# A fused two-block kernel: its modulation front in one piece per channel tile, sums by transposes, parameters loaded later

## The reference

```python
c_act = jax.nn.silu(c)
mod = (c_act @ w_mod[l] + b_mod[l])[:, None, :]
sh1, sc1, g1, sh2, sc2, g2 = jnp.split(mod, N_MOD, axis=-1)
h = rms_norm(x) * (1.0 + sc1) + sh1
proj = h @ w_in[l]
```

## Time and profile before

| | |
|---|---|
| median of 3 runs | 1368.52 us (1367.58 to 1370.42) |
| profiled execution: its time | 1368.94 us |
| profiled execution: span, first to last instruction | 1367.6 us |
| TensorE busy | 1354.0 us (99%) |
| VectorE, ScalarE, GpSimd busy | 896.1, 629.1, 241.8 us |
| DMA moved, mean | 163.46 MB, 120 GB/s |
| mean granted TensorE clock | 0.999 |

### The profile page before, as it was taken

The page is one execution under the profiler, slowest core; times in us unless marked ns, Lnnn a source line. Parts: engine busy times, 40 slices in busy tenths (PEclk is TensorE's granted clock), DMA queues, the critical chain, the costliest instruction groups (busy, mean ns, idle before and its releaser), DMA issues.

```text
span 1367.6 us, 24510 instructions
## 1 busy us (share of the span) xinstructions
PE 1354.0 (99%) x9502; PEld 1094.6 (80%) x9502; DVE 896.1 (66%) x1274; ACT 629.1 (46%) x1000; POOL 241.8 (18%) x254
## 2 busy tenths in 40 slices
PE   8999999999999999999999999999999999999998
PEld 5788888888887888878888888888888877777776
DVE  4687877887658867775668543234444687777865
ACT  4566556565555522332245441223333465545533
POOL 0000000000028889770022600000000000000320
PEclk9999999999999999999999999999999999999999
DMA  9444444444455676463333333333333232223221
GB/s 347 131 141 138 118 123 131 120 127 124 143 142 154 159 205 206 146 177 92 93 93 92 108 93 105 96 93 92 96 105 92 73 106 67 80 60 93 64 74 77
DMA packets 276009, 163.46 MB, mean 120 GB/s; under 512 B 6573, under 2 KB 264242, under 8 KB 275898
## 3 DMA queue, kind: packets, MB, share of 16 engines
q1 hardware_dynamic: 269530, 158.90, 40.1%
q10 hardware_dynamic: 6368, 3.00, 0.8%
HBM read 159.59 MB, written 2.29 MB: 118 GB/s over the span
## 4 chain that ended last, share of the span: by engine, by line
PE 89%; DVE 4%; ACT 2%; issue 2%; POOL 2%; DMA 1%; ACTq 0%; SPq 0%; DVEq 0%; POOLq 0%
PE PS L742 23%; PE PS L744 22%; PE PS L743 22%; PE PS L942 1%; PE PS L1354 1%; PE PS L1019 1%; PE PS L1021 1%; PE PS L1020 1%; POOL mbuf L607 1%; PE PS L963 1%; PE PS L1355 1%; PE PS L1356 1%; PE PS L1257 1%; PE PS L1268 1%; POOL mbuf L602 1%
## 5 line engine op out<-in xcount | busy, mean ns | idle before, releaser
L742 PE MATMUL PS<-Hh,whi 128*128 128x512 f32 x1096 | 443.1, 404 | 1.0 <-DVE wlo L2114 0.5
L744 PE MATMUL PS<-Hh,wlo 128*128 128x512 f32 x1096 | 427.7, 390 | 0.0
L743 PE MATMUL PS<-Hl,whi 128*128 128x512 f32 x1096 | 427.3, 390 | 0.0
L2114 DVE TENSOR_TENSOR wlo<-raw,whi 128x1024 fp32r<-128x1024 f32 (+2 forms) x211 | 275.7, 1307 | 119.3 <-ACT whi L1457 118.5
L1457 ACT ACTIVATE whi<-raw 128x1024 fp32r<-128x1024 f32 (+2 forms) x215 | 222.6, 1036 | 168.7 <-PE PS L744 119.0
L742 PEld LDWEIGHTS PS<-Hh,whi 128*128 128x128 f32 x1096 | 205.8, 188 | 49.9 <-issue 6.2
L744 PEld LDWEIGHTS PS<-Hh,wlo 128*128 128x128 f32 x1096 | 205.7, 188 | 44.4
L743 PEld LDWEIGHTS PS<-Hl,whi 128*128 128x128 f32 x1096 | 206.1, 188 | 39.6 <-issue 0.7
L602 POOL TENSOR_TENSOR mbuf<-mbuf,cact 128x1024 f32<-128x1024 f32 x32 | 67.1, 2097 | 409.6 <-DMA mbuf<-in_w_mod_dram 403.6
L607 POOL TENSOR_TENSOR mbuf<-mbuf 128x512 f32<-128x512 f32 x68 | 101.8, 1497 | 5.3
L742 PE MATMUL PS<-YBh,whi 128*128 128x512 f32 x256 | 99.6, 389 | 0.0
(11 more groups left out here) (484 smaller groups left out, 1957.9 us busy)
## 6 DMA issues: line engine op xcount, KB each, us to landing
raw<-in_w_in_dram SPq DMA_DIRECT2D x106, 512.0 KB, 3.9
raw<-in_w_ff_dram SPq DMA_DIRECT2D x64, 512.0 KB, 3.7
mbuf<-in_w_mod_dram SPq DMA_DIRECT2D x32, 512.0 KB, 3.9
crow<-cum_rows SPq DMA_DIRECT2D x32, 256.0 KB, 4.4
...
```

What stands on the lines that cost most here:

```text
L742: pe.matmul(bank[:, :], whi[s][:, k, :], xh[:, kk, :], start=kk == 0, stop=False)
L743: pe.matmul(bank[:, :], whi[s][:, k, :], xl[:, kk, :], start=False, stop=False)
L744: last = pe.matmul(bank[:, :], wlo[s][:, k, :], xh[:, kk, :], start=False, stop=t == end - 1 and k == (order or range(kt))[-1])
L2114: v.tensor_tensor(wlo[s][:, 0:kt, :], raw[s][:, 0:kt, :], whi[s][:, 0:kt, :].bitcast(F32), ALU.subtract).then_inc(s_wlo, 1)
```

## The change

- The columns of `w_mod` are loaded in eight pairs, one per channel tile m: `wm[m]` takes the 128 scale columns and the 128 shift columns of tile m, two loads of 128 columns each. `mod_rows(m)` takes both in one go, 256 wide, eight times (before: four times 128 and six times 256).
- `mod_sums(m)` turns both halves of `mrow` by two transposes; VectorE adds the four partial sums by a reduction over 4 of the columns that it picks (partitions 0, 32, 64, 96 of before), into two new columns of `small`, and then makes `opc` and `modc` for one channel tile. `selc` and its three GpSimd instructions fall away.
- At the start ScalarE issues only `c` and `b_mod`, without a wait between, and runs one Silu on a constant ahead of that of `c`. The other five loads of `fill1` go to SyncE, ahead of the ten of `fill2`, behind the last landing of `wm`. Their transposes and copies stand at the end of the front.
- The order on TensorE, ScalarE and VectorE is written anew: 10 fillers at the start become 4, all four chunks of x are turned in one go, the first `mod_rows` waits until x is copied whole, the parts of channel tile m - 1 stand around `mod_rows(m + 1)` and so on. `lo(2)` stands behind `h_scaled(2)`. The last parts are one channel tile's for each of the three tiles (before: two channel tiles').
- The unused filler tensor and its GpSimd copies go; `small` grows by as much as `selc` took with its padding, and all other buffers keep their places. Waits on shared semaphores are counted anew.

The diff, cut to its core (left out are the waits that were only counted anew):

```diff
-    selc = sb("selc", [P, 2])
...
-    small = sb("small", [P, 64])
+    small = sb("small", [P, 72])
...
-    N_PAR2 = 16 * 10
+    N_BMOD, N_PAR2 = 16, 16 * 16
...
-    MOD_ROWS = [(i, at, 128) for at in (0, 128) for i in (4, 0)] + [(j + i, 0, 256) for j in range(1, 4) for i in (4, 0)]
-    of_cols = lambda m: m if m < 2 else m // 2 + 1
...
-        def load_mod0(i, at, n):
-            if at:
-                sp.wait_ge(s_x[i // 4], 16)
-            sp.dma_start(wm[i][:, :, at:at + n], cols(W_MOD, i * 256 + at, n)).then_inc(s_wmr[i // 4] if at else s_wm[i], 16)
+        def load_mod0(m):
+            for j in (1, 0):
+                sp.dma_start(wm[m][:, :, j * 128:j * 128 + 128], cols(W_MOD, j * D + m * 128)).then_inc(s_wm[m], 16)
 
         for c in range(NC):
             load_x(c)
-        for p, piece in enumerate(MOD_ROWS):
-            load_mod0(*piece)
-            if p in (1, 3, 5):
-                load((1, 3, 5).index(p))
-
-        sp.wait_ge(s_wm[3], 16)
-        for to, ap in fill2:
+        for m in range(KT):
+            load_mod0(m)
+            if m < 3:
+                load(m)
+
+        sp.wait_ge(s_wm[7], 32)
+        sp.wait_ge(s_par2, N_BMOD)
+        for to, ap in fill1[2:] + fill2:
...
-        def keep_busy_rounded(n, width, bank=5):
-            for i in range(n):
-                pe.matmul(BK[bank][:, 0:width], filler[:, i % 2 * 128:i % 2 * 128 + 128], filler[:, 0:width],
-                          start=True, stop=True)
-
-        def keep_busy_half(n, bank=5):
+        def keep_busy_half(n, bank=2):
+            pe.wait_ge(s_const, 6)
...
-                    pe.wait_ge(s_pc, 3)
+                    pe.wait_ge(s_cact, 1)
...
-        keep_busy(4, 0)
         pe.wait_ge(s_par, 16)
         pe.transpose(BK[5][:, 0:8], pr[1][0:8, :], ident[0:8, 0:8]).then_inc(s_pt, 1)
-        keep_busy(6, 0)
-        x_turned(0)
-        x_turned(1)
-        pe.wait_ge(s_par, 16 * 7)
-        pe.wait_ge(s_cact, 1)
-        pe.transpose(BK[5][:, 128:256], pr[1][:, :], ident[:, :]).then_inc(s_pt, 1)
-        x_turned(2)
-        x_turned(3)
-
-        def mod_rows(n):
-            i, at, width = MOD_ROWS[n]
-            if n >= 2:
-                pe.wait_ge(s_mrow, n - 1)
-            pe.wait_ge(*((s_wmr[i // 4], 32) if at else (s_wm[i], 16)))
+        keep_busy(4, 0)
+        for c in range(NC):
+            x_turned(c)
+
+        def mod_rows(m):
+            if m >= 2:
+                pe.wait_ge(s_mrow, m - 1)
+            pe.wait_ge(s_wm[m], 32)
             for k in range(KT):
                 q = 32 * (k % 4)
-                ms = pe.matmul(BK[3 + n % 2][q:q + 32, 0:width], cact[:, k:k + 1].to_broadcast([P, 32]),
-                               wm[i][:, k, at:at + width], start=k < 4, stop=k >= 4)
+                ms = pe.matmul(BK[3 + m % 2][q:q + 32, 0:256], cact[:, k:k + 1].to_broadcast([P, 32]), wm[m][:, k, :],
+                               start=k < 4, stop=k >= 4)
             ms.then_inc(s_mt, 1)
 
-        def mod_sums(n):
-            pe.wait_ge(s_mrow, n + 1)
-            if n >= 2 and n % 2 == 0:
-                pe.wait_ge(s_modc, n)
-            for to, at in [(2 * (n % 2) + n // 2, 0)] if n < 4 else [(2 * n - 4, 0), (2 * n - 3, 128)]:
-                ms = pe.matmul(BK[6][:, to:to + 1], mrow[n % 2][:, at:at + 128], selc[:, 0:1], start=True, stop=True)
+        def mod_sums(m):
+            pe.wait_ge(s_mrow, m + 1)
+            if m > 0:
+                pe.wait_ge(s_modc, 2 * m)
+            for j in range(2):
+                ms = pe.transpose(BK[6][:, j * 128:j * 128 + 128], mrow[m % 2][:, j * 128:j * 128 + 128], ident[:, :])
             ms.then_inc(s_ms, 1)
...
+        pe.wait_ge(s_xt1, 2)
+        pe.wait_ge(s_par2, N_BMOD)
+        pe.transpose(BK[5][:, 128:184], pr[1][0:56, :], ident[0:56, 0:56]).then_inc(s_pt, 1)
+        pe.wait_ge(s_xt0, 6)
+        keep_busy_half(4)
+        mod_rows(0)
+        keep_busy_half(3)
+        mod_sums(0)
+        keep_busy_half(5)
         mod_rows(1)
-        pe.wait_ge(s_xt1, 2)
-        keep_busy(2, 5)
-        mod_sums(0)
+        part(0, 0)
         mod_sums(1)
-        keep_busy_half(6)
+        keep_busy_half(9)
         mod_rows(2)
-        keep_busy_half(3)
-        mod_rows(3)
-        pe.wait_ge(s_xt0, 6)
-        part(0, 0)
-        mod_sums(2)
-        mod_sums(3)
-        keep_busy_half(9)
         part(1, 0)
         part(0, 1)
+        mod_sums(2)
         part(1, 1)
+        part(2, 0)
+        mod_rows(3)
+        part(2, 1)
+        mod_sums(3)
+        part(0, 2)
+        part(1, 2)
         mod_rows(4)
+        part(2, 2)
+        mod_sums(4)
+        part(0, 3)
+        part(1, 3)
         mod_rows(5)
-        keep_busy_half(2)
-        mod_sums(4)
+        part(2, 3)
         mod_sums(5)
-        keep_busy_half(4)
-        part(2, 0, 1)
+        part(0, 4)
+        part(1, 4)
         mod_rows(6)
-        part(0, 2, 3)
+        part(2, 4)
+        mod_sums(6)
+        part(0, 5)
+        part(1, 5)
         mod_rows(7)
-        part(1, 2)
-        mod_sums(6)
+        part(2, 5)
         mod_sums(7)
-        part(1, 3)
-        part(2, 2, 3)
-        mod_rows(8)
-        part(0, 4)
-        mod_rows(9)
-        part(0, 5)
-        mod_sums(8)
-        mod_sums(9)
-        part(1, 4, 5)
-        part(2, 4, 5)
+        part(0, 6)
+        part(1, 6)
+        part(2, 6)
         pe.wait_ge(s_par2, N_PAR2)
-        pe.transpose(BK[3][:, :128], pr[0][:, :], ident[:, :]).then_inc(s_pt, 1)
+        pe.transpose(BK[3][:, 0:128], pr[0][:, :], ident[:, :]).then_inc(s_pt, 1)
+        pe.transpose(BK[3][:, 128:256], pr[1][:, :], ident[:, :]).then_inc(s_pt, 1)
         pe.transpose(BK[4][:, :rC], pr[2][0:rC, :], ident[0:rC, 0:rC]).then_inc(s_pt, 1)
         for t in range(3):
-            part(t, 6, 7)
+            part(t, 7)
...
-        act.wait_ge(s_par, 16)
-        for to, ap in fill1[1:]:
-            act.dma_start(to, ap).then_inc(s_par, 16)
+        act.dma_start(*fill1[1]).then_inc(s_par2, 16)
+        act.wait_ge(s_pc, 1)
+        act.activation(small[:, 63:64], EPS, ACTF.Silu)
...
-        mod_row(0)
-        mod_row(1)
-        hi(0)
-        h_hi(0)
-        mod_row(2)
-        mod_row(3)
-        hi(1)
-        h_hi(1)
-        mod_row(4)
-        mod_row(5)
-        hi(2)
-        for j in range(1, 4):
-            h_hi(2 * j)
-            h_hi(2 * j + 1)
-            for n in ((6, 7), (8, 9), ())[j - 1]:
-                mod_row(n)
+        for m in range(KT):
+            mod_row(m)
+            if m < 3:
+                hi(m)
+            h_hi(m)
...
-        for b in range(2):
+        for b in range(4):
             x_copy(b, 0)
-        v.wait_ge(s_pt, 2)
-        cols_of(BK[5][:, 128:256], pcB, 128, 1.0)
-        for b in range(2, 4):
-            x_copy(b, 0)
-        x_copy(0, 1)
         v.wait_ge(s_rx, 5)
         v.reciprocal(small[:, 4:8], small[:, 4:8]).then_inc(s_xrs, 1)
+        x_copy(0, 1)
         x_copy(2, 1)
-
-        def h_cols(i):
-            m, n = (i, 1) if i < 2 else (2 * i - 2, 2)
-            at = m if i < 2 else 2 * m
-            v.wait_ge(s_ms, 2 * i + 2)
-            v.scalar_tensor_tensor(out=opc[:, m:m + n], in0=BK[6][:, at:at + n], scalar=1.0,
-                                   in1=colr("b_mod", 8 + m, n), op0=ALU.add, op1=ALU.add).then_inc(s_modc, 1)
-            v.tensor_tensor(modc[:, m:m + n], BK[6][:, at + 2:at + 2 + n], colr("b_mod", m, n),
-                            ALU.add).then_inc(s_modc, 1)
+        v.wait_ge(s_pt, 2)
+        cols_of(BK[5][:, 128:184], pcB, 56, 1.0)
+
+        def h_cols(m):
+            total = small[:, 32:34]
+            v.wait_ge(s_ms, m + 1)
+            own(v.tensor_reduce(total, BK[6][:, 0:256].rearrange("p (b g r) -> p b g r", g=4, r=32)[:, :, :, 0],
+                                mybir.AxisListType.X, ALU.add))
+            v.wait_ge(s_dve, nown)
+            v.scalar_tensor_tensor(out=opc[:, m:m + 1], in0=total[:, 1:2], scalar=1.0, in1=col("b_mod", 8 + m),
+                                   op0=ALU.add, op1=ALU.add).then_inc(s_modc, 1)
+            v.tensor_tensor(modc[:, m:m + 1], total[:, 0:1], col("b_mod", m), ALU.add).then_inc(s_modc, 1)
...
+        for m in range(KT):
             h_cols(m)
             h_scaled(m)
-            lo(m)
+            if m < 3:
+                lo(m)
             h_lo(m)
-        lo(2)
-        for j in range(1, 4):
-            h_cols(j + 1)
-            h_scaled(2 * j)
-            h_scaled(2 * j + 1)
-            h_lo(2 * j)
-            h_lo(2 * j + 1)
-        v.wait_ge(s_pt, 3)
+        v.wait_ge(s_pt, 4)
         cols_of(BK[3][:, 0:128], pcA, 128, 0.5)
-        v.wait_ge(s_pt, 4)
+        v.wait_ge(s_pt, 5)
         cols_of(BK[4][:, 0:rC], pcC, rC, 1.0)
-        v.tensor_scalar(colr("conv_b", 0, 32), colr("conv_b", 0, 32), 0.5, None, ALU.mult).then_inc(s_pc, 1)
-        v.tensor_scalar(colr("ssm_norm_w", 0, 16), colr("ssm_norm_w", 0, 16), 0.5, None, ALU.mult).then_inc(s_pc, 1)
```

(6 more changed lines are left out.)

46 lines of the change are left out of this document (17 added, 29 removed).

## The result

| | before | after |
|---|---|---|
| median of 19 runs each, same chip | 1367.95 us (1367.35 to 1370.42) | 1370.44 us (1368.85 to 1372.07) |
| ratio, 95% interval | | 1.0016 (1.0010 to 1.0023) |
| profiled execution: span | 1367.6 | 1369.2 |
| the handover (first full projection matmul) | 50.45 (L742) | 51.77 (L731) |
| step 19 of the `dt` chain (first matmul that reads `dts`) | 64.94 (L918) | 67.16 (L900) |

The change made the kernel 0.16% slower. The time lies in the predicted range, but the interval leaves out "no change", so the forecast was wrong by some 2 us. The last row says where to look: 1302.04 is 1369.2 - 67.16, and the same subtraction for the kernel before gives no less. So all that this execution lost is there at 67 us.

What follows compares the result with a forecast made beforehand. The prediction took the front, ending at the handover behind ScalarE's `dt` copy, to set the time, with TensorE nearly gapless after. Handover 50.4 against 50.45 meant no change: profiled 1368.9, median 1368.4 us, range 1367.2 to 1371.3.

Steps and rivals of the forecast that it cites:

- The loads: Front's DMA: 16 column halves and 3 raw tiles at 346 GB/s, 1.515 us each, last landing at 37.1.
- The starved part: Front from the first `mod_rows` at 12.3 to `part(2, 0)` at 25.9, with TensorE waiting on landings and VectorE.
- P: Start of `part(2, 0)` on TensorE, forecast at 25.9, behind a gap of 1 to 2 us.
- The full part: Front from `part(2, 0)` on: TensorE without waits until the last channel tile, 3.68 per cycle, front ending at 48.8.
- clock rival: Start of the front: fewer fillers leave TensorE at half clock, 2.85 us more, 1371.3 (or 1372.2); 12 in 100.
- The handover: First full projection matmul, behind ScalarE's splits and `dt` copy: forecast 50.4 against 50.45, no change.
- Parameters: Small loads moved to SyncE: fifteen at 0.35 each end at 42.4; raw tiles 3 to 5 land at 46.2 to 49.5.
- late parameters: Rival, SyncE's queue: small requests at 0.45 each delay raw tile 4 and the `dt` copy, 0.8 more, 1369.2; 12 in 100.
- signs of being wrong: First fillers behind x 0.43 apart, `part(t, 7)` awaiting parameters, raw tile 4 behind 49, or a longer stretch behind 51 us.
- Off the path: Work said to cost nothing: GpSimd's missing instructions, small VectorE copies, and `dt_bias` requests at 46.9 instead of 46.17.
- 0.8 of the 1.78 is used: Later `dt_bias` requests use 0.8 of the 1.78 us between L1561's end and the matmul at 62.04 needing its bank.

Runs made afterwards that it cites:

- act_params: Kernel after the change, with all fifteen small parameter requests issued by ScalarE instead of SyncE, raw tiles right behind the last columns: median 1368.65 us, ratio 1.0004.
- after_bc_early: Kernel after the change, with `dt_bias` and its neighbours requested without waiting for the parameter columns, their users not waiting for `gm_bs`: median 1370.00 us, ratio 1.0012.
- before_bc_late: Kernel before the change, with one added wait that puts its `dt_bias` requests to 48.24, as late as in the kernel after: median 1370.61 us, ratio 1.0016.

## Why the prediction was wrong

**The loads.** Right in rate from 9 to 16 and 31 to 36 (344 for 346), short in the sum: the last columns let SyncE go on at 38.75, not at 37.2. From 23 to 32 the rate was 316, and x landed some 0.5 later than taken.

**The starved part.** Right. The first `mod_rows` at 12.73 (forecast 12.3), the reduction 0.17 long, the low end of its bounds, P at 26.64 (25.9) with the forecast pause ahead of it.

**The full part.** The cycle was shorter, 3.51 for 3.68 (L803 at 32.67, 36.18, 39.69 and 43.21 in the chain of waits); the one under the fallen clock took 5.09 (27.58 to 32.67), 1.6 more. That TensorE would run at full clock from P on had been taken without giving a reason. `mod_rows(7)` began 4.4 behind its landing, as forecast. What I had not seen is the clock falling in the middle: the prediction's clock rival was a cold start, and that did not come (fillers 0.22 apart at 11.76, 11.99, 12.21, 12.42).

**The handover.** The working was right: the last part's last matmul begins at 50.13, TensorE waits 1.24 for ScalarE's `dt` copy. But it came at 51.77, not 50.4, from two causes of about one size, either of which is enough: the clock (act_params: raw tiles early, handover 51.56) and the late raw tiles (after_bc_early: clock at 1.00, handover 51.44).

**The step that failed** is the one under *Parameters*: "Fifteen from 37.2 on end at 42.4", with raw tiles landing "at 46.2, 47.8 and 49.5". They began at 38.75, took 0.42 each and not 0.35, ended at 44.98, and the tiles landed between 48.7 and 51.7, over 2 later. Of the 2.6 by which they ended late, 1.6 is the late start and 1.0 the price of the requests. In the prediction's sum raw tile 4 had 0.8 to spare, so either was enough. The rival *late parameters* had the mechanism (0.45 each, counting from 0.05 on) with 12 in 100; the runs bear it out, with the late start beside it that it did not have. Two of the prediction's own signs of being wrong came: raw tile 4 landed behind 49, and the stretch behind 51 us grew, from the handover to step 19 by 0.9 (15.39 for 14.49). The rival's price, 0.8, was too low, because of a second step:

**Off the path.** "0.8 of the 1.78 is used" took L1561 as the first that suffers. The chain of the same four loads has a longer branch, through VectorE to step 19 (L918), whose cover was nearly nothing. I had followed the branch to the bank and not the branch to `dts`. The kernel after waits 0.87 there, and with the same delay put into the kernel before (before_bc_late) TensorE waits 1.60 at that matmul. The request itself came at 48.40, not 46.9, since it stands behind the end of the front, 1.6 late by the clock. And request times were compared where the landing decides: `gm_bs`, asked for among the late raw tiles, took 6.28.

That the time lay in the range all the same is no merit of the sum: its upper end was the price of a cold start, which did not come.
